# Loads, squares and sums reordered ahead of a projection, with the compression of cached rows moved between its steps

## The reference, cut to what matters

```
sh1, sc1, gt1, sh2, sc2, gt2 = ada_mod(c, ada_w, ada_b)      # silu(c) @ ada_w + ada_b, 6 parts of 1024
h = rmsnorm(x, norm1_g) * (1.0 + sc1) + sh1
xr, yg, q, kv_c, kv_s, kv_w, gl = split_columns(h @ w_in)    # 18 groups of 128 columns, and 24 gates
# cached rows of 8 samples: 64 pages of 128 rows, compressed by blocks of 32 rows with stride 16
past_c = cache_cmp[layer, page_table]
proj = chunk_proj(past_c, cmp_w1)                            # rows @ w1
hid = pos @ w1 + proj[0] + proj[1]
ck = gelu(hid) @ w2                                          # compressed keys and values
...                                                          # three attention branches, recurrence
x = x + gt1 * mixed
x = x + gt2 * peer_ffn(h2)                                   # 16384 experts: by far the longest part
```

## Time and profile before

| what | value |
|---|---|
| three runs, median | 1976.24 us (1966.25 to 1976.55) |
| profiled execution | 1976.61 us |
| its span, first to last instruction | 1974.9 us |
| PE busy | 1827.0 us (93%) |
| DVE busy | 1356.8 us (69%) |
| ACT busy | 642.4 us (33%) |
| mean granted TensorE clock | 0.959 |
| HBM read and written | 406.46 and 64.14 MB |

### The profile page before, as it was taken

The page is one execution under the profiler, slowest core; times in us unless marked ns, Lnnn a source line. Parts: engine busy times, 40 slices in busy tenths (PEclk is TensorE's granted clock), DMA queues, the critical chain, the costliest instruction groups (busy, mean ns, idle before and its releaser), DMA issues.

```text
span 1974.9 us, 30075 instructions
## 1 busy us (share of the span) xinstructions
PE 1827.0 (93%) x11287; PEld 1673.9 (85%) x11287; DVE 1356.8 (69%) x2913; ACT 642.4 (33%) x1009; POOL 338.0 (17%) x362
## 2 busy tenths in 40 slices
PE   3899997978879997999999999999999999999996
PEld 2778884544668997999999999999999999999995
DVE  0302422366337778999989999996777777777775
ACT  1112431057213222333334334333333333333331
POOL 1220010000000000111123333332222222222220
PEclk9799997979999999999999999999999999999998
DMA  8736562310033222766779999998999999999981
GB/s 279 240 99 218 199 221 95 156 58 1 0 121 130 88 77 62 230 227 225 236 238 331 359 361 344 343 342 319 397 401 341 338 340 340 341 337 336 336 276 44
DMA packets 177133, 465.41 MB, mean 236 GB/s; under 512 B 20217, under 2 KB 91129, under 8 KB 175476
## 3 DMA queue, kind: packets, MB, share of 16 engines
q1 hardware_dynamic: 132148, 289.72, 42.4%
q0 software_dynamic: 44864, 174.14, 24.5%
HBM read 406.46 MB, written 64.14 MB: 238 GB/s over the span
## 4 chain that ended last, share of the span: by engine, by line
PE 75%; DVE 16%; DMA 3%; SPq 3%; issue 2%; ACT 2%; DVEq 0%; ACTq 0%
PE ps L1006 28%; PE ps L903 17%; PE ps L526 7%; PE ps L890 5%; PE ps L987 4%; PE ps L853 3%; DVE ul L1618 2%; PE ps L582 1%; DVE xT L1661 1%; ACT arena L1040 1%; DMA arena<-rrows 1%; PE ps L829 1%; SPq L278 1%; DVE arena L1703 1%; DVE arena L1701 1%
## 5 line engine op out<-in xcount | busy, mean ns | idle before, releaser
L1618 DVE TENSOR_TENSOR ul<-raw,uh 128x1024 fp32r<-128x1024 f32 x256 | 311.3, 1222 | 130.4 <-ACT uh L1040 128.7
L903 PE MATMUL ps<-hh,uh 128*128 128x392 f32 x1024 | 360.4, 352 | 22.8 <-DVE ul L1618 22.7
L1006 PE MATMUL ps<-ah,uh 128*128 128x392 f32 x1024 | 348.1, 340 | 3.4 <-DVE al L1806 3.4
L1006 PE MATMUL ps<-ah,ul 128*128 128x392 f32 x1024 | 350.4, 342 | 0.0
L903 PE MATMUL ps<-hl,uh 128*128 128x392 f32 x1024 | 350.3, 342 | 0.0
L1006 PE MATMUL ps<-al,uh 128*128 128x392 f32 x1024 | 349.8, 342 | 0.0
L903 PE MATMUL ps<-hh,ul 128*128 128x392 f32 x1024 | 349.5, 341 | 0.0
L1040 ACT ACTIVATE uh<-raw 128x1024 fp32r<-128x1024 f32 x256 | 270.1, 1055 | 113.3 <-PE ps L1006 103.3
L488 POOL DMA_INDIRECT xT<-in_u,gidx x128 | 149.4, 1167 | 611.4 <-DVE zg L1661 379.6
L903 PEld LDWEIGHTS ps<-hh,uh 128*128 128x128 f32 x1024 | 193.9, 189 | 29.6 <-DVE ul L1618 28.1
L488 POOL DMA_INDIRECT xT<-in_v,gidx x128 | 133.0, 1039 | 418.5 <-DVE vacc L1796 384.3
(11 more groups left out here) (335 smaller groups left out, 2321.4 us busy)
## 6 DMA issues: line engine op xcount, KB each, us to landing
raw<-in_uT SPq DMA_DIRECT2D x128, 512.0 KB, 5.1
raw<-in_v SPq DMA_DIRECT2D x128, 512.0 KB, 6.3
zs<-zbuf SPq DMA_DIRECT2D x128, 196.0 KB, 5.4
gw<-stage POOLq DMA_DIRECT2D x28, 896.0 KB, 9.6
gr<-gw SPq DMA_DIRECT2D x32, 784.0 KB, 8.2
zin<-zs SPq DMA_DIRECT2D x128, 196.0 KB, 5.8
arena<-in_ada_w SPq DMA_DIRECT2D x32, 512.0 KB, 4.2
arena<-in_w_in SPq DMA_DIRECT2D x18, 512.0 KB, 4.4
```

What stands on the lines that cost most here:

```text
L903: last = mm(ps[:, bank, 0:DN], w[x][:, k * P:(k + 1) * P], m[:, k, G0:TOK], start=(k == 0 and x == 0 and m is hh), stop=(k == KD - 1 and x ...
L1006: last = mm(ps[:, dc, 0:DN], w[:, q, cols], m[:, q, :], start=(first and w is uh and m is ah), stop=(final and w is ul))
L1618: tt(ul[:, i % 4, :], raw[:, i % 4, :], uh[:, i % 4, :].bitcast(F32), SUB).then_inc(S["lo_done"], 1)
```

## The change

On SP, x and the tables that the modulation needs (`par`, `adab`, relative biases, `oha`, `ohd`, and the broadcast relative biases `rbx`) get a semaphore of their own, `tables_loaded`, and stand early; the last of the six is issued behind the fourth modulation load, which waits for the first step. The first two projection weights and the gate weights come before the cached pages. SP loads pages 0 to 15 before the projection and pages 16 to 31 in its loop pass n = 2, ahead of the weights of step 3. Its pages of selected rows start at n = 7, three per pass. POOL's cached pages wait for the third modulation step, and its broadcast of the bias rows comes behind all 32 of them.

On PE the relative-bias row moves from the very start into modulation step 3. Step 0 needs only its weights; after it PE waits for the tables, does bias group 0 and the sum of squares, and then goes on with steps 1 to 3. On DVE `normed` follows the first turned part, and only `shifted` follows the last. The gate matmuls and the projection come right behind; the compression (`hidden_pages(0)`, `hidden_pages(1)`, `keys_pages`) follows the fifth step (n = 4), and `values_pages` stands in step 5, with the banks of PSUM that this needs. Step 0 waits for the bias row to be moved out, step 1 for the bias groups, and step 6 instead of step 1 for the values. No matmul is added or removed.

```diff
             load(cT, io["cT"], S["c_loaded"])
             load_head(0, 0)
-            load(ohd[0:33], io["ohd"], S["small_loaded"])
-            load(oha[0:33], io["oha"], S["small_loaded"])
-            load(rb[0:32], io["rel_bias"], S["small_loaded"])
+            load(xT[:, :, :], io["xT"], S["x_loaded"])
+            load(par[:, 0:80], io["par"], S["tables_loaded"])
+            load(par[:, 80:128], io["adab"], S["tables_loaded"])
+            load(rb[0:32], io["rel_bias"], S["tables_loaded"])
+            load(oha[0:33], io["oha"], S["tables_loaded"])
+            load_head(1, 1)
+            load(ohd[0:33], io["ohd"], S["tables_loaded"])
+            load_head(2, 2)
+            sp.wait_ge(S["ada_ready"], 1)
+            load_head(3, 0)
             load(rbx[0:32].rearrange("p (b h) -> p b h", h=NH),
-                 io["rel_bias"].rearrange("a (o h) -> a o h", o=1).to_broadcast([32, NB, NH]), S["small_loaded"])
-            load_head(1, 1)
-            load(par[:, 0:80], io["par"], S["small_loaded"])
-            load(par[:, 80:128], io["adab"], S["small_loaded"])
-            load(xT[:, :, :], io["xT"], S["x_loaded"])
-            load_head(2, 2)
+                 io["rel_bias"].rearrange("a (o h) -> a o h", o=1).to_broadcast([32, NB, NH]), S["tables_loaded"])
+            load(wgate, io["w_gate"], S["wgate_loaded"])
             load(newmask[0:ROWS], io["newmask"], S["small_loaded"])
             load(gsum[0:ROWS], io["gsum"], S["small_loaded"])
             load(validq, io["validq"], S["small_loaded"])
             load(blkno[0:ROWS, 0:NSELB], io["blkno"], S["small_loaded"])
-            sp.wait_ge(S["ada_ready"], 1)
-            load_head(3, 0)
-
-            sp.wait_ge(S["page_loaded"], 16)
-            for n in range(32):
-                page_rows(sp, xpool[:, n, :], io["pool_c"], n, S["gather_k"])
-                if n == 7:
-                    load(w1p, io["w1p"], S["w1k_loaded"])
-                    load(posp, io["posp"], S["pos_loaded"])
-                    sp.wait_ge(S["prep_done"], 1)
-                    for c in range(2):
-                        for g in range(2):
-                            load(w2[g * HD:(g + 1) * HD, c, g * HD:(g + 1) * HD], io["cmp_w2"][c], S["w2_loaded"])
-            sp.wait_ge(S["ada_ready"], ADA_HEAD)
-            load(wgate, io["w_gate"], S["wgate_loaded"])
+            sp.wait_ge(S["ada_ready"], 3)
             for n in range(2):
                 load(win_w[:, n * KD:(n + 1) * KD, :], io["w_in"][n], w_l[n])
+            load(w1p, io["w1p"], S["w1k_loaded"])
+            load(posp, io["posp"], S["pos_loaded"])
+            sp.wait_ge(S["prep_done"], 1)
+            for c in range(2):
+                for g in range(2):
+                    load(w2[g * HD:(g + 1) * HD, c, g * HD:(g + 1) * HD], io["cmp_w2"][c], S["w2_loaded"])
+            sp.wait_ge(S["page_loaded"], 16)
+
+            def load_pages(a, b):
+                for n in range(a, b):
+                    page_rows(sp, xpool[:, n, :], io["pool_c"], n, S["gather_k"])
+            load_pages(0, 16)
 
             def load_tail(i):
                 if i >= 2:
                     sp.wait_ge(S["ada_ready"], ADA_HEAD + i - 1)
                 load(ada_tail[i % 2], io["ada_w"][16 + i], ada_l[i % 2])
-            load_tail(0)
-            load_tail(1)
             load(stc, io["state_conv"], S["lrus_loaded"])
...
             for n in range(2, ZC):
                 sp.wait_ge(S["z_ready"], n - 1)
                 load(win_w[:, (n % 2) * KD:(n % 2 + 1) * KD, :], io["w_in"][n], w_l[n % 2])
+                if n == 2:
+                    load_tail(0)
+                    load_tail(1)
+                    load_pages(16, 32)
                 if n >= 3:
                     load_tail(2 * n - 4)
                     load_tail(2 * n - 3)
...
+                if n < 7:
+                    continue
                 sp.wait_ge(S["hid_ready"], 2)
-                for q in range(2):
-                    m = 2 * (n - 2) + q
+                for m in range(3 * (n - 7), min(3 * (n - 6), 32)):
                     page_rows(sp, sel[:, m, :], io["pool_s"], m, S["gather_s"])
...
-            pool.wait_ge(S["act_init"], 2)
-            pool.dma_start(rscratch, rsb[0:NH]).then_inc(S["scratch_stored"], 16)
             pool.wait_ge(S["page_loaded"], 16)
+            pool.wait_ge(S["ada_ready"], 3)
             for n in range(32, 64):
                 page_rows(pool, xpool[:, n, :], io["pool_c"], n, S["pages_k"])
-                if n == 40:
-                    pool.wait_ge(S["scratch_stored"], 16)
-                    rows = io["rrows"]
-                    pool.dma_start(rows.rearrange("p h c -> p (h c)"),
-                                   rscratch.rearrange("h (o c) -> o (h c)", o=1).to_broadcast([P, NH * 640])
-                                   ).then_inc(S["rows_stored"], 16)
+                if n == 39:
+                    pool.wait_ge(S["act_init"], 3)
+                    pool.dma_start(rscratch, rsb[0:NH]).then_inc(S["scratch_stored"], 16)
+            pool.wait_ge(S["scratch_stored"], 16)
+            rows = io["rrows"]
+            pool.dma_start(rows.rearrange("p h c -> p (h c)"),
+                           rscratch.rearrange("h (o c) -> o (h c)", o=1).to_broadcast([P, NH * 640])
+                           ).then_inc(S["rows_stored"], 16)
...
-            pe.wait_ge(S["small_loaded"], 160)
-            pe.wait_ge(S["prep_done"], 2)
-            mm(ps[0:NH, 0, 0:512], rb[0:33], ohd[0:33, 513:1025], start=True, stop=True)
-            mm(ps[0:NH, 1, 0:128], rb[0:33], ohd[0:33, 1025:1153], start=True, stop=True).then_inc(S["pe_init"], 1)
...
-                    pe.wait_ge(S["act_init"], 2)
+                    pe.wait_ge(S["z_moved"], 4)
                 else:
-                    pe.wait_ge(S["gelu_ready"], 1)
+                    pe.wait_ge(S["m9_ready"], ADA_HEAD + 6)
                 xv = xpool.rearrange("p (h a) (c g j n) -> p h a c g j n", h=2, c=2, g=2, n=8)
+                b = 2 + 2 * c
                 for h in range(2):
                     for m in range(2):
                         for j in range(8):
                             for g in range(2):
-                                mm(ps[g * HD:(g + 1) * HD, h, 1 - m:257 - m], w1p[:, c * 16 + m * 8 + j, :],
+                                mm(ps[g * HD:(g + 1) * HD, b + h, 1 - m:257 - m], w1p[:, c * 16 + m * 8 + j, :],
                                    xv[:, h, :, c, g, j, :], start=(m == 0 and j == 0), stop=(m == 1 and j == 7),
...
+                pe.wait_ge(S["z_moved"], 5)
...
                 ada_step(g, lambda k: aw[:, :, k, :], 512)
-                if g:
-                    turn_m9(g - 1)
+                if g == 0:
+                    pe.wait_ge(S["tables_loaded"], 96)
+                    offset_bias(0)
+                    pe.wait_ge(S["act_init"], 2)
+                    two(0, lambda k: ones[:, :], lambda k: hT[:, k, :], range(KD)).then_inc(S["sum_ready"], 1)
+                    continue
+                turn_m9(g - 1)
+                if g == 3:
+                    pe.wait_ge(S["root_in"], 1)
+                    mm(ps[0:NH, 0, 0:512], rb[0:33], ohd[0:33, 513:1025], start=True, stop=True)
+                    mm(ps[0:NH, 1, 0:128], rb[0:33], ohd[0:33, 1025:1153], start=True, stop=True).then_inc(S["pe_init"], 1)
                 offset_bias(g)
             turn_m9(ADA_HEAD - 1)
-            pe.wait_ge(S["act_init"], 3)
-            pe.wait_ge(S["m9_ready"], ADA_HEAD)
-            two(4, lambda k: ones[:, :], lambda k: hT[:, k, :], range(KD)).then_inc(S["sum_ready"], 1)
-            pe.wait_ge(S["prep_done"], 4)
-            hidden_pages(0)
-            keys_pages()
-            hidden_pages(1)
...
-            values_pages()
...
+                if n == 0:
+                    pe.wait_ge(S["act_init"], 3)
                 if n == 1:
+                    pe.wait_ge(S["prep_done"], 4)
+                if n == 6:
                     pe.wait_ge(S["ck_moved"], 2)
...
+                if n == 5:
+                    pe.wait_ge(S["gelu_ready"], 2)
...
+                if n == 5:
+                    values_pages()
...
+                if n == 4:
+                    hidden_pages(0)
+                    hidden_pages(1)
+                    keys_pages()
...
-            act.wait_ge(S["pe_init"], 1)
-            act.wait_ge(S["act_init"], 1)
-            link(fn(rsb[0:NH, 0:512], ps[0:NH, 0, 0:512], ACT.Copy))
-            fn(rsb[0:NH, 512:640], ps[0:NH, 1, 0:128], ACT.Copy).then_inc(S["act_init"], 1)
...
             copy_m9(0)
-            copy_m9(1)
             act.wait_ge(S["x_loaded"], 16)
             fn(hT, xT[:, :, :], ACT.Square).then_inc(S["act_init"], 1)
+            copy_m9(1)
+            root(1)
             copy_m9(2)
+            act.wait_ge(S["pe_init"], 1)
+            link(fn(rsb[0:NH, 0:512], ps[0:NH, 0, 0:512], ACT.Copy))
+            fn(rsb[0:NH, 512:640], ps[0:NH, 1, 0:128], ACT.Copy).then_inc(S["act_init"], 1)
```

(77 more changed lines are left out.)

## The result

| | changed | before |
|---|---|---|
| median of 7 runs | 1991.17 us (1989.55 to 1995.55) | 1974.75 us (1966.25 to 1978.34) |
| ratio, 95% interval | 1.0096 (1.0082 to 1.0109) | |
| profiled execution | 1995.55 us, span 1993.9 | 1976.61 us, span 1974.9 |

The kernel is slower by 0.96%, which is 19.0 us on a median of 1974.75; the two medians are 16.4 us apart. The forecast time, 1991.5, fits the median to 0.3 us. That it fits so closely is luck: the forecast shift was +15.2 us, the profile has +21.0 us at the last projection step, since one wait had been priced at nothing, and the median before came out 1.5 us lower over seven runs than over the first three.

What follows compares the result with a forecast made beforehand. PE bounds the kernel after the start, so its arrival at the projection decides: -31.3 + 36.0 + 7.9 + 2.3 + 0.9 - 0.6 = +15.2 us. Against the median of 1976.24 that gives 1991.4; forecast 1991.5 us, range 1980 to 2000.

Steps and rivals of the forecast that it cites:

- last table lands: SP's six small tables, now behind a fourth 2048 KB load: last landing at 34.0 us instead of 29.45, +4.3 us.
- PE from there to turn 3: PE from bias group 0 at 34.1 us to the last turned modulation part: 46.5 us, ending at 80.6.
- bias 0, sums, step 1: First PE stages after the tables: bias group at slow price 6.1 us, sum of squares 9.5, modulation step 1.8.
- h exposed; gate matmuls: After the last turn, 5.2 us of VectorE work uncovered by PE; gate matmuls 7.10 us plus 2.4 for the cold start.
- projection step 0: Start of the first projection step on PE: 95.3 us, 31.3 us earlier than before.
- work put back, with the wait for the values: Compression, keys and values between projection steps: +36.0 us, including 0.5 for step 6's wait and 0.6 for work switches.
- wait and cold restart at step 3: PE stalls 7.9 us for weights behind 16 page rows on SP's queue, then restarts after idling, +2.3 us.
- last weights later: SP's three selected-row pages per step delay each later weight load by 1.1 us; the last costs PE +0.9 us.
- full-clock rival: PE keeps clock 1.00 from the sums to the projection: total -5.0 us, 1971.6 us; chance 0.07.
- the choice that the prediction left open: Modulation steps on PE: either they gain nothing from full clock, or the level shown before the first matmuls was wrong.
- POOL's selected pages start near 180 and need 25 us; PE wants them after 300: hidden.: POOL's loads of selected pages during the projection, claimed to add no time.
- broadcast rival: POOL's 2560 KB bias-row broadcast still runs at 121 us, delaying step 3's weights 10 us: +25, 2001.8 us; chance 0.10.

Runs made afterwards that it cites:

- e2: Changed kernel with ohd and the broadcast bias table rbx issued ahead of the second modulation load; ratio to before 1.0026.
- e4: Changed kernel with the relative-bias row and last bias group placed behind the last turned modulation part on PE, beside VectorE's shift; ratio to before 1.0093.
- e7: e1 with POOL's 2560 KB broadcast of the bias rows moved behind the last projection step; ratio to before 1.0051.
- e3: Changed kernel with POOL's load of the compression weights issued ahead of its 21 selected pages; median 1990.65 us, ratio to before 1.0073.
- e1: Changed kernel with all 32 of SP's cached pages issued ahead of the projection, none in loop pass n=2; ratio to before 1.0088.
- e6: Changed kernel with the edits of e1, e2, e3 and e4 together, and POOL's bias-row broadcast behind the projection; ratio to before 0.9951.
- e8: e6 with SP's cached pages split, 24 ahead of the projection and 8 in loop pass n=2; median 1955.99 us, ratio to before 0.9916.

## Why the prediction was right, and where it was not

| step of the prediction | forecast | profile |
|---|---|---|
| last table lands | 34.0 | 33.9 |
| PE from there to turn 3 | 46.5 | 45.7 (33.91 to 79.63) |
| bias 0, sums, step 1 | 6.1, 9.5, 1.8 | 6.1, 9.1, 1.9 |
| h exposed; gate matmuls | 5.2; 9.5 | 5.2; 8.9 |
| projection step 0 | 95.3 | 93.7 |
| work put back, with the wait for the values | 36.0 | 35.8 |
| wait and cold restart at step 3 | 7.9 + 2.3 | 8.9 + 1.9 |
| wait for the weights of step 8 | 0 | 5.5 + 2.1 |
| last weights later | 0.9 | 0.4 |
| last step against before | +15.2 | +21.0 |

**Right.** The view that decided it was PE's stages with their clocks, set beside SP's queue. Moved work was counted as the same work (36.0 for 35.8); what mattered were the covers it lost: idle PE at the tables, the shift of h, and the weights behind 16 page rows. e2, e4 and e7 took these one by one and gave back 14.2, 3.7 (8.0 at its place) and 10.2 us. The full-clock rival fell: bias group 2 again took 6.07 us at clock 0.50, with PE busy throughout.

```profile
61.43:67.50 6.07, 6.07 (x29) 6.04 (x28) 0.35 (x2) 0.00 (x0) 3.02 (x6) 0.50 0.88 336
```

Its one true part is step 1 behind the sums, which took 1.85 us, half of the 3.57 us of a step at clock 0.50. This bears on the choice that the prediction left open: a step can take half as long, so the first one, at 3.4 us under a shown 1.00, most likely did not have the full clock.

**Wrong, one step.** "POOL's selected pages start near 180 and need 25 us; PE wants them after 300: hidden." The pages were hidden, but I costed only who waits for them, not what they and the load behind them meet. POOL's compression weights, 1 MB at the end of that row, used to go out at about 143 us and now went out at 201, 0.2 us behind the weights of step 8. PE wanted those 7.2 us after their issue, so by the usual 4.4 us they had 2.8 us of slack, and they took 12.7. The price is 7.6 us: 5.5 of wait and 2.1 of slower running in step 8. e3 showed it, by moving only that load. A small slip of reading beside it: the prediction calls the chain of the kernel before "PE without a break" behind 80.70 us, but it passes over ScalarE for some 2.5 us ahead of L594 and over SP and the landing of weights at 166 to 176 us. The sum counts both places, so nothing in it hangs on this.

**Half right.** The broadcast rival (10 us if the broadcast meets weights of the projection) was priced well and timed well: issued at 103.6, it was over at 117.1 (119 forecast), before the weights of step 3 at 121.56, but only because SP's queue kept those back. e1 made the two meet: the weights took 12.7 us, 8.5 more than in e7, and the queue's gain was gone but for 1.7 us.

The sum of the misses is +7.6, less 1.6 from the earlier start of step 0 and small terms: 21.0 instead of 15.2. The measured 19.0 us by the ratio and 16.4 by the medians lie below the 21.0, within what one profile of each kernel can tell. So the direction, the terms and the waits were forecast; the 0.3 us between forecast and median were not earned, because a miss of 7.6 us stands in the sum.

## What to carry to other kernels

When work is moved between the steps of a loop that loads its own weights, write down the issuing queue of each step: here every page row of 128 KB was 1.1 to 1.2 us of the queue ahead of the next weights. A small table that gates an engine belongs ahead of the megabytes, and a wait that disappears must be followed to the next one: here the second cover was a broadcast, the third a 1 MB load. Test such edits together as well as alone, since of two causes in series the first showed nearly nothing when it alone was removed (e1).

## What the runs showed of the hardware

- The same 512 KB load landed in 4.4 us (median) in the kernel before, in 12.7 us beside two 512 KB loads that POOL issued 0.2 us later, and one of the modulation loads in 16.5 us beside a 2560 KB broadcast. In the last 9 us of the first case the 16 DMA engines were busy for 0.99 of the time but moved only 227 GB/s, where the first loads moved 413 GB/s at a share of 1.02. So the engines' time was full, though the bytes were few; why these transfers take so much of it was not tried.

```profile
205.00:213.95 8.95, 3.43 (x45) 2.62 (x44) 0.00 (x0) 6.41 (x9) 0.00 (x0) 0.85 0.99 227
```

- Ahead of about 52 us the shown clock of the changed kernel is 1.00 while bias group 0 takes 6.07 us, its half-clock price. Ahead of the first change of the clock in a trace, the rows' clock is not to be read as the array's speed:

```profile
33.91:39.98 6.07, 6.07 (x29) 6.05 (x29) 0.00 (x0) 0.00 (x0) 0.00 (x0) 1.00 0.00 0
```

- The stretch from the last projection step to the end was 1684 to 1697 us long in the eleven profiles. The late broadcast lies in it in e6, e7 and e8; the other eight, in which no edit touches it, span the same range. In its first 200 us the granted clock was 0.87 in the two shortest (e2 and e7) and 0.82 to 0.84 in the five longest. A single profile's total can't judge an edit of 5 us here; a landmark close behind the edit can.
